# The recurrent block's gate products as three fp32r products of halves that POOL makes

## What is computed

```python
def rglru_block(x, w_in, conv_w, conv_b, w_a, b_a, w_i, b_i, lam, w_out):
    xb, gb = jnp.split(x @ w_in, [D_RNN], axis=-1)
    xb = causal_dwconv(xb, conv_w, conv_b)                    # 4 taps
    xh = xb.reshape(bsz, s, N_BLOCKS_B, BLOCK_B)              # 8 blocks of 128 channels
    r  = jax.nn.sigmoid(jnp.einsum("bsnc,ncd->bsnd", xh, w_a) + b_a)
    ig = jax.nn.sigmoid(jnp.einsum("bsnc,ncd->bsnd", xh, w_i) + b_i)
    log_a = -LRU_C * r * jax.nn.softplus(-lam)
    a, mult = jnp.exp(log_a), jnp.sqrt(-jnp.expm1(2.0 * log_a))
    u = mult * (ig * xb)
    _, hseq = lax.associative_scan(combine, (a, u), axis=1)   # h = a*h + u along the positions
    return (hseq * jax.nn.gelu(gb)) @ w_out
```

## Time and profile before

| quantity | value |
|---|---|
| median of 3 runs | 1261.48 us (1260.67 to 1262.12) |
| profiled execution: its own time | 1261.65 us |
| profiled execution: span | 1259.9 us |
| PE busy | 1252.0 us, 99% of the span |
| POOL busy | 861.3 us, 68% |
| DVE busy | 537.0 us, 43% |
| ACT busy | 408.9 us, 32% |
| mean granted TensorE clock | 1.00 |

### The profile page before, as it was taken

How to read it: one execution, slowest core, us unless ns; L and a number is a source line. 1 busy time by engine, 2 the same in 40 slices (tenths; PEclk the granted TensorE clock), 3 DMA queues, 4 the chain that set the end, 5 groups by cost and what they waited for, 6 DMA issues and landing times.

```text
span 1259.9 us, 17776 instructions
## 1 busy us (share of the span) xinstructions
PE 1252.0 (99%) x5893; PEld 1021.6 (81%) x5893; DVE 537.0 (43%) x832; ACT 408.9 (32%) x683; POOL 861.3 (68%) x1155
## 2 busy tenths in 40 slices
PE   9999999999999999999999999999999999999998
PEld 5777778788888888888888778888888888888887
DVE  6545545465344444201343375274444443301352
ACT  4445444224333434100144384014343433200041
POOL 7544557819877877777577646929877788777573
PEclk9999999999999999999999999999999999999999
DMA  5222132303322233333243222312222224333221
GB/s 196 69 67 67 52 115 89 112 17 109 108 88 95 100 122 111 110 92 100 67 167 103 81 84 84 117 51 100 100 100 100 91 93 133 118 100 94 74 92 59
DMA packets 57294, 120.63 MB, mean 96 GB/s; under 512 B 3761, under 2 KB 36081, under 8 KB 56737
## 3 DMA queue, kind: packets, MB, share of 16 engines
q1 hardware_dynamic: 56192, 117.45, 28.3%
q10 hardware_dynamic: 1056, 2.58, 0.6%
HBM read 117.83 MB, written 2.20 MB: 95 GB/s over the span
## 4 chain that ended last, share of the span: by engine, by line
PE 97%; DMA 1%; DVE 1%; ACT 1%; DVEq 0%; issue 0%; ACTq 0%; SPq 0%
PE bank L437 19%; PE bank L439 19%; PE bank L438 19%; PE bank L456 8%; PE bank L457 8%; PE bank L458 8%; PE bank L731 2%; PE bank L738 2%; PE bank L733 2%; PE bank L564 1%; PE bank L551 1%; PE bank L465 1%; PE bank L521 1%; PE bank L523 1%; DMA x<-xT 1%; PE bank L907 1%
## 5 line engine op out<-in xcount | busy, mean ns | idle before, releaser
L423 POOL TENSOR_TENSOR w_lo<-stage,w_hi 128x256 fp32r<-128x256 f32 x800 | 593.7, 773 | 29.5 <-issue 1.5
L417 POOL TENSOR_SCALAR w_hi<-stage 128x1024 fp32r<-128x1024 f32 x200 | 213.4, 1067 | 175.3 <-PE bank L458 77.3
L437 PE MATMUL bank<-x_hi,w_hi 128*128 128x512 f32 (+1 forms) x712 | 275.6, 387 | 0.0
L439 PE MATMUL bank<-x_hi,w_lo 128*128 128x512 f32 (+1 forms) x712 | 275.3, 387 | 0.0
L438 PE MATMUL bank<-x_lo,w_hi 128*128 128x512 f32 (+1 forms) x712 | 275.3, 387 | 0.0
L438 PEld LDWEIGHTS bank<-x_lo,w_hi 128*128 128x128 f32 x712 | 133.7, 188 | 27.3
L437 PEld LDWEIGHTS bank<-x_hi,w_hi 128*128 128x128 f32 x712 | 133.7, 188 | 27.1
L439 PEld LDWEIGHTS bank<-x_hi,w_lo 128*128 128x128 f32 x712 | 133.7, 188 | 26.9
L1150 DVE SCALAR_TENSOR_TENSOR tmp<-bank,cols,tmp 128x511 f32<-128x511 f32 x88 | 66.0, 750 | 201.3 <-ACT tmp L1431 190.3
L415 POOL TENSOR_TENSOR waiter<-waiter 128x1 f32<-128x1 f32 x101 | 21.1, 209 | 171.3 <-PE bank L439 119.0
L456 PE MATMUL bank<-w_hi,h_hi 128*128 128x512 f32 x352 | 137.3, 390 | 0.0
(11 more groups left out here) (182 smaller groups left out, 1806.5 us busy)
## 6 DMA issues: line engine op xcount, KB each, us to landing
stage<-w_square SPq DMA_DIRECT2D x163, 512.0 KB, 3.2
stage<-w_down SPq DMA_DIRECT2D x44, 512.0 KB, 3.6
rows<-norm_rows SPq DMA_DIRECT2D x4, 1024.0 KB, 6.2
outT<-x SPq DMA_DIRECT2D x7, 256.0 KB, 2.0
x<-xT SPq DMA_DIRECT2D x3, 512.0 KB, 6.9
p_in<-pT ACTq DMA_DIRECT2D x2, 512.0 KB, 3.4
w_ai<-w_lru SPq DMA_DIRECT2D x1, 1024.0 KB, 9.4
stage<-w_square ACTq DMA_DIRECT2D x1, 512.0 KB, 7.2
```

The lines of the kernel that those rows point to most:

```text
L417: whole = pool.tensor_scalar(high[:, s, :], stage[:, s, :], 1.0, 0.0, ALU.mult, ALU.add)
L423: piece = pool.tensor_tensor(low[:, s, to], stage[:, s, to], high[:, s, to].bitcast(F32), ALU.subtract)
L437: pe.matmul(out, w_hi[:, s, c:c + P], m_hi, start=first, stop=False)
L439: return pe.matmul(out, w_lo[:, s, c:c + P], m_hi, start=False, stop=last)
```

## The change

POOL gets three new duties, PE's gate products become six matmuls for a tile in place of two, and the gates wait for POOL in place of DVE. The other engines' programs are unchanged. The four new tiles have space of their own behind `emb`.

```diff
@@ sbuf
         emb = place("emb", [P, KT, SEQ], F32, a)
+        w_ai_hi = place("w_ai_hi", [P, KT, 2 * P], F32R, a)
+        w_ai_lo = place("w_ai_lo", [P, KT, 2 * P], F32R, a)
+        conv_hi = place("conv_hi", [P, 2, SEQ], F32R, a)
+        conv_lo = place("conv_lo", [P, 2, SEQ], F32R, a)
@@ gpsimd
-            for ph in phases.values():
+            def split_gate_weights():
+
+                pool.wait_ge(lru_w_loaded, 16)
+                for m in range(0, KT, 2):
+                    pool.tensor_scalar(w_ai_hi[:, m:m + 2, :], w_ai[:, m:m + 2, :], 1.0, 0.0, ALU.mult, ALU.add)
+                    pool.drain()
+                    pool.tensor_tensor(w_ai_lo[:, m:m + 2, :], w_ai[:, m:m + 2, :],
+                                       w_ai_hi[:, m:m + 2, :].bitcast(F32), ALU.subtract).then_inc(lru_w_split, 1)
+
+            def split_convolved(m):
+
+                pool.wait_ge(rg_conv, m + 1)
+                if m >= 2:
+                    pool.wait_ge(rg_gates, m - 1)
+                pool.tensor_scalar(conv_hi[:, m % 2, :], conv_x[:, m % 4, :], 1.0, 0.0, ALU.mult, ALU.add)
+                pool.drain()
+                pool.tensor_tensor(conv_lo[:, m % 2, :], conv_x[:, m % 4, :], conv_hi[:, m % 2, :].bitcast(F32),
+                                   ALU.subtract).then_inc(rg_conv_split, 1)
+
+            for name, ph in phases.items():
+                if name == "rgx":
+                    split_gate_weights()
                 for i in rounds(pool, ph):
                     for r, place_at in enumerate(ph.slots):
...
                         piece.then_inc(unit_split, 1)
+                        if name == "rgx" and r >= 4:
+                            split_convolved(r - 4)
+                        if name == "rgg" and r < 3:
+                            split_convolved(r + 4)
+                        if name == "rgg" and r == 2:
+                            split_convolved(KT - 1)
@@ tensor
             def rg_gate_products(m):
-                pe.wait_ge(rg_conv, m + 1)
+                pe.wait_ge(rg_conv_split, m + 1)
                 if m >= 2:
                     pe.wait_ge(rg_sig, m - 1)
                     pe.wait_ge(rg_input, m - 1)
                 bank = 2 + 2 * (m % 2)
-                pe.matmul(banks[bank][:], w_ai[:, m, 0:P], conv_x[:, m % 4, :], start=True, stop=True)
-                pe.matmul(banks[bank + 1][:], w_ai[:, m, P:2 * P], conv_x[:, m % 4, :], start=True,
-                          stop=True).then_inc(rg_gates, 1)
+                for gate in range(2):
+                    to, at = banks[bank + gate][:], slice(gate * P, (gate + 1) * P)
+                    pe.matmul(to, w_ai_hi[:, m, at], conv_hi[:, m % 2, :], start=True, stop=False)
+                    pe.matmul(to, w_ai_lo[:, m, at], conv_hi[:, m % 2, :], start=False, stop=False)
+                    mm = pe.matmul(to, w_ai_hi[:, m, at], conv_lo[:, m % 2, :], start=False, stop=True)
+                mm.then_inc(rg_gates, 1)
...
-            pe.wait_ge(lru_w_loaded, 16)
+            pe.wait_ge(lru_w_split, KT // 2)
```

More of the change, by code:

```diff
@@ L281, in hybrid_trunk_kernel @@
             sem(n) for n in ("p_loaded", "p_hi_ready", "p_lo_ready", "gated", "emb_added"))
-        lru_w_loaded = sem("lru_w_loaded")
+        lru_w_loaded, lru_w_split, rg_conv_split = sem("lru_w_loaded"), sem("lru_w_split"), sem("rg_conv_split")
         lam_exp, lam_abs = sem("lam_exp"), sem("lam_abs")
```

## The result

Thirteen runs of each kernel: 1264.68 us (1262.95 to 1266.22) after the change, 1262.35 us (1260.59 to 1263.98) before. The ratio is 1.0021, 95% interval 1.0014 to 1.0028: the changed kernel is slower, by 2.3 us in the medians. The profiled execution has a span of 1262.7 us, 2.8 above that of before; 0.65 of it arises long ahead of the block (rgx 0's first matmul starts at 687.89, against 687.24 in the earlier trace rows), where a wait for a DMA takes 1.3 us in place of 0.7. I therefore measure the block from that matmul.

A forecast was written before the change was run, and what follows sets the result against it. PE was taken as the bound from end to end; -3.2 us for products, +4.1 for the wait at gates 7 and +0.1 rounding gave +1.0, so 1262.5 us against a median of 1261.48, range 1261.2 to 1265.2.

The forecast's parts named there:

- the sum: Whole kernel: -3.2 us for cheaper gate products, +4.1 for PE's wait at gates 7, +0.1 rounding, net +1.0 us.
- the first rival: PE's standstill ahead of gates 7 lowers its clock, costing 1.5 us more: 1264.0 us, or 1265.5; chance 0.20.
- What PE saves: Gate products on PE: six fp32r matmuls take 1.36 us against 1.76, saving 0.40 us a tile, 3.2 for eight.
- POOL's costs: New splits on POOL: 2.05 us each, bounds 1.9 to 3.3; gate weights 8.2 us ahead of rgx 0, hidden.
- Tiles 0 to 6: Gates of convolved tiles 0 to 6: POOL's halves are ready in time, so PE does not wait.
- The shift of convolution 7: DVE's last convolution, through chains of ACT and DVE, comes 0.8 us earlier, ending at 749.19; range 0.4 to 1.6.
- The wait: Ahead of gates 7, PE stands still 4.1 us for POOL's split of tile 7; rgg 1 starts 1.0 us later.
- The clock, the step that failed: PE behind the pause at gates 7: clock stays at full speed, as activity lies right before and behind it.
- About 0.2% is what a measurement can tell.: Whole kernel: differences up to about 0.2% (2.5 us) cannot be told from no change.
- 0.81 on no change: Whole kernel: chance 0.81 of the same time within 2.5 us, against 0.05 faster and 0.14 slower.

The follow-up runs named there:

- the repetition: The changed kernel run again unaltered, in the third group, beside the kernel before: 1266.12 us, ratio 1.0018.
- The kernel that has no pause: Changed kernel with convolution 7 behind scan 2 on DVE and sigmoids 6 and 7 ahead of decays 4 on ACT: 1259.38 us, ratio 0.9979.
- the fp32 kernel with the hop: Changed kernel with POOL's splits and the gates' wait for them kept, but gates computed with the two fp32 products of before: 1263.35 us, ratio 1.0015.
- the first reordered kernel: Changed kernel with only DVE's order altered, convolution 7 behind scan 2 and drives 4 and 5 ahead of scan 3: 1266.52 us, ratio 1.0029.
- the fp32 control: Kernel before, with fp32 products and no new POOL work, given the new orders of DVE and ACT: 1262.22 us, ratio 1.0001.
- group two: The second group of four follow-up kernels, run on one chip beside the kernel before, which measured 1262.31 us there.

## Why the prediction was right, and where it was not

The range (1261.2 to 1265.2) held the time, and the sum had the right sign (+1.0). But the case that happened is the first rival, which had 0.20, not the forecast, which had 0.68.

That the range held owes something to luck. The sum started from a median of 1261.48 us for the kernel before, which was 1262.35 in the comparison. And the changed kernel's thirteen executions lie on both sides of the range's upper end: the median, 1264.68, falls among those at a clock of 0.999, while four at 0.997 are at 1266.1 to 1266.2. In the repetition the median itself, 1266.12, is outside.

- **What PE saves.** 0.40 us a tile was right. The kernel that has no pause shows 3.0 of the 3.2 us in its trace and 2.8 in the medians.
- **POOL's costs.** 2.05 us for a split; measured 0.62 + 0.15 + 1.29 = 2.06. The gate weights: 8.2, measured 8.1, hidden as said.
- **Tiles 0 to 6.** No wait for their halves. One small thing was missed: gates 6 start some 0.2 us late (rows 746.65 and 747.07 of PE, 0.42 apart in place of 0.23). The row names no releaser; DVE's drive 4, which gates 6 wait for, ends at about 746.95.
- **The shift of convolution 7.** 0.8 us; measured 0.81. That scan 1 would now be what ACT's decays wait for shows in the row at 735.01, idle 0.76 for DVE's state.
- **The wait.** Predicted 4.1 us and a net +1.0. Measured 3.5 us from the last matmul to the next, and +0.8 in the trace whose clock stayed. The arrival of PE was 0.2 later, and the hop, from the end of convolution 7 at 749.83 to PE's first row at 752.03, took 2.2 us in place of 2.54. The stated bounds of this part were also added wrongly: a shift of 1.6 and a split of 1.9 give 1.0 - 0.8 - 0.15, that is about 0, and not -0.2.
- **The clock, the step that failed.** The forecast left it at full speed, on the ground that PE is active right before and behind the pause and that no row tells otherwise. It fell in the profiled execution and, by the mean clock of 0.997, in seven of eleven of the repetition. The price for one loss was right: 1.5 us from the start's rows, 1.4 in the profile after. In the profile of the repetition it is 1.6, since all of its slow stretch has matmuls in it, while in the first the clock fell during the pause. The sum with it, +0.8 + 1.4 = +2.2, is what the two profiles show from rgx 0 on; the medians' +2.3 agrees because, by clock and time, the median execution of the change has one loss; that the one of before, at 1262.35, has none is inferred from its time alone. The Trainium skill (TensorE: Matmul & The Clock Gate, HAM oscillation) had warned of such pauses; the trace agrees, with 0.50 from 752 to 755 us, and a larger chance ought to have followed from it.
- **"About 0.2% is what a measurement can tell."** With 0.81 on no change by that bound the estimate was too sure: 1.0021 lies at its edge, with an interval of 0.0007 to either side.

The cause is shown, not only argued: filling the pause takes the clock's part away, the fp32 kernel with the hop keeps the wait without the saving, and moving the convolution and the sigmoids gives 3.0 of the 3.2 us. The medians hold clock losses near the start too. The time from rgx 0's first matmul to the end of the span leaves them out. Against the 572.7 us of before it is as follows in the profiled executions:

| kernel | us against before | granted clock behind the pause |
|---|---|---|
| changed | +2.2 | low |
| changed, repeated | +2.4 | low |
| pause filled with 13 | +0.8 | 1.00 |
| pause filled with 5 | +2.4 | low |
| fp32 products behind the split | +1.9 | 1.00 |
| tile 7 in fp32 | -0.9 | 1.00 |
| rgg 1 ahead of gates 7, both times | -1.3 | 1.00 |
| convolution 7 earlier | +3.1 | low |
| the same order in the kernel before | +2.5 | 1.00 |
| both orders changed | -3.0 | 1.00, no pause |
| both orders, fp32 products | 0.0 | 1.00, no pause |

What stays open is why the clock survives in some executions, two of eleven in the repetition; the program is the same in all.

## What to carry to other kernels

When an engine that bounds the kernel gets cheaper work, ask at each place where it now arrives first what it meets there, and walk its releaser's chain back to where that chain is tied to something that did not move. A last tile with no other work between its preparation and its use is the place to look at first: here the hop over one more engine was hidden in every tile but that one. A pause on TensorE can have a second price that its length does not show. Filling it with 13 matmuls took that price away here, and with 5 it did not; doing other work first, as with rgg 1 ahead of gates 7, took most of the pause itself. And an order that is changed on one engine must be followed through the queue of the engine that waits for it, as the two kernels with only DVE's order changed show: they lose 2.5 us with the clock kept and 3.1 with it lost, from rgx 0 on.

## What was not expected of the hardware

A pause of TensorE shorter than that of the change can cost the clock, but does not always. It stood still for 2.3 us in the kernel with the pause filled in part and ran at 1.2 GHz behind it. An equal pause of 2.3 us, in the kernel before with DVE's new order, left the clock at 1.00, and so did 1.6 us in the fp32 kernel behind the splits and the pauses of 1.2 us (ahead of rgg 1 in two profiles, ahead of gates 7 in one). These are single profiled executions, so no length can be named as the bound.

The moment of the fall differs too. In the first profile of the change the granted clock falls within the pause (0.83 from 751 to 752 us, 0.50 from 752). In its repetition and in the kernel filled in part it falls when PE has been at work again for about half a us: 1.00 and 0.98 from 753 to 754, 0.54 and 0.50 from 754 to 755.

Near the start PE also waits for a DMA (`k_a` from forget_rows), 0.7 us in the profile of before and 1.3 in that of the change. In the later groups it was 1.5 to 1.7 us, and the clock over 30 to 60 us was 0.94 in five of those profiles (both kernels with PE's order or the pause changed in these groups, the repetition, the first reordered kernel and the fp32 control) and 1.00 in two (1.5 us in the fastest kernel, 1.7 in the kernel before with DVE's order). Where it was lost, rgx 0 starts at 689.3 to 689.4 us, and in the two others at 687.8 and 688.0: some 1.4 us for this loss. The same wait thus costs the clock in one execution and not in another. This part need not come from the change: the fp32 control has it, and about a quarter of the executions of the kernel before look like it (7 of 27 in group two lie at 1263.6 us or more, with a mean clock of 0.998 or 0.999), though none of those was profiled. A comparison of a thousandth therefore needs many executions of both kernels, or distances between two fixed points of the traces.
